# Where four operand splits and the feature splits stand in two engines' programs, at the start of a feed-forward stage

## The reference, cut to what matters

```python
h = rms_norm_2(x, norm2[l])
gate, up = jnp.split(h @ w_ffn_in[l], 2, axis=-1)
x = x + (jax.nn.silu(gate) * up) @ w_ffn_out[l]
return rms_norm_2(x, final_norm)
```

## Time and profile before

| | |
|---|---|
| median of 3 runs | 2473.76 us (2472.62 to 2474.74) |
| profiled execution, its own time | 2474.8 us |
| its span, first to last instruction | 2473.5 us |
| TensorE busy | 2366.0 us (96% of the span) |
| VectorE busy | 1412.2 us (57%) |
| ScalarE busy | 1138.8 us (46%) |
| GpSimd busy | 894.1 us (36%) |
| mean granted TensorE clock | 0.988 of full |

### The profile page before, as it was taken

The page is one execution under the profiler, slowest core; times in us unless marked ns, Lnnn a source line. Parts: engine busy times, 40 slices in busy tenths (PEclk is TensorE's granted clock), DMA queues, the critical chain, the costliest instruction groups (busy, mean ns, idle before and its releaser), DMA issues.

```text
span 2473.5 us, 31358 instructions
## 1 busy us (share of the span) xinstructions
PE 2366.0 (96%) x12068; PEld 1949.2 (79%) x12068; DVE 1412.2 (57%) x1963; ACT 1138.8 (46%) x1778; POOL 894.1 (36%) x665
## 2 busy tenths in 40 slices
PE   4999999989999999999999999999999999999998
PEld 3778788868888878876678877788877888888886
DVE  5255489958885240129973743332476666666665
ACT  4322288868884231239962474132333333333334
POOL 0111233336652212326521222012256655556551
PEclk8999999999999999999999999999999999999999
DMA  7234300000003131100021311013111111111111
GB/s 293 81 118 132 116 5 1 1 19 1 1 1 111 35 123 51 43 9 1 10 103 43 106 53 43 26 35 116 47 52 51 52 52 52 52 51 52 55 57 68
DMA packets 152488, 143.23 MB, mean 58 GB/s; under 512 B 10358, under 2 KB 140692, under 8 KB 150420
## 3 DMA queue, kind: packets, MB, share of 16 engines
q1 hardware_dynamic: 152340, 141.22, 18.1%
HBM read 124.43 MB, written 16.78 MB: 57 GB/s over the span
## 4 chain that ended last, share of the span: by engine, by line
PE 80%; ACT 8%; issue 5%; DVE 4%; POOL 2%; DMA 0%; SPq 0%; ACTq 0%; DVEq 0%; POOLq 0%
PE ps L260 37%; PE ps L2588 14%; PE ps L2605 9%; PE ps L1083 4%; PE ps L1106 3%; PE ps L1093 3%; ACT C_PR L1753 1%; PE ps L1642 1%; ACT B_PR L1166 1%; POOL WSL L2505 1%; ACT B_PTH L1160 1%; PE ps L2564 1%; PE ps L1621 1%; ACT C_PTH L1761 1%; PE ps L2032 1%
## 5 line engine op out<-in xcount | busy, mean ns | idle before, releaser
L249 POOL TENSOR_TENSOR WL<-WR,WH 128x1024 fp32r<-128x1024 f32 (+1 forms) x89 | 207.1, 2327 | 840.2 <-ACT WH L244 840.0
L260 PE MATMUL ps<-HH,WH 128*128 128x512 f32 (+1 forms) x1136 | 363.2, 401 | 3.3 <-POOL WL L249 1.7
L260 PE MATMUL ps<-HL,WH 128*128 128x512 f32 (+1 forms) x1136 | 353.4, 392 | 0.0
L260 PE MATMUL ps<-HH,WL 128*128 128x512 f32 (+1 forms) x1136 | 352.7, 392 | 0.0
L260 PEld LDWEIGHTS ps<-HH,WH 128*128 128x128 f32 (+1 forms) x1136 | 209.6, 189 | 56.2 <-issue 10.1
L260 PEld LDWEIGHTS ps<-HL,WH 128*128 128x128 f32 (+1 forms) x1136 | 213.8, 188 | 47.4
L260 PEld LDWEIGHTS ps<-HH,WL 128*128 128x128 f32 (+1 forms) x1136 | 213.7, 188 | 47.3
L2818 DVE TENSOR_TENSOR XF<-ps,XF 128x1024 f32<-128x1024 f32 x168 | 201.5, 1220 | 32.5 <-PE ps L2605 25.8
L2588 PE MATMUL ps<-HC,WSH 128*128 128x512 f32 x640 | 197.0, 389 | 0.0
L1119 DVE TENSOR_REDUCE NM<-ps 128x1 f32<-128x1024 f32 x128 | 156.1, 1220 | 35.0 <-PE ps L1083 34.1
L2505 POOL TENSOR_TENSOR WSL<-WSR,WSH 128x512 fp32r<-128x512 f32 x100 | 131.5, 1315 | 107.6 <-ACT WSH L2499 107.6
(11 more groups left out here) (432 smaller groups left out, 5217.1 us busy)
## 6 DMA issues: line engine op xcount, KB each, us to landing
WS<-in_w_ffn_in SPq DMA_DIRECT2D x44, 512.0 KB, 5.1
MKW<-in_ada_w SPq DMA_DIRECT2D x32, 512.0 KB, 4.1
spill<-X SPq DMA_DIRECT2D x3, 4096.0 KB, 13.6
OW<-in_w_ffn_out SPq DMA_DIRECT2D x22, 512.0 KB, 3.5
WR<-in_w_in SPq DMA_DIRECT2D x20, 512.0 KB, 3.9
WR<-in_odd_w_in SPq DMA_DIRECT2D x19, 512.0 KB, 3.8
WR<-in_even_w_in SPq DMA_DIRECT2D x17, 512.0 KB, 5.0
AWK<-in_ada_w SPq DMA_DIRECT2D x8, 1024.0 KB, 9.8
```

The lines of the kernel that those rows point to most:

```text
L249: pool.tensor_tensor(low[:, :, :], raw[:, :, :], high[:, :, :].bitcast(F32), ALU.subtract).then_inc(*w_low.up(t))
L260: last = pe.matmul(ps[0:w.m, 2 * s + h, :], wt[:, k, :], x[:, k, halves(h)], start=(k == 0 and n == 0), stop=(k == w.kt - 1 and n == 2))
```

## The change

Two groups of steps move within ScalarE's and VectorE's programs. No instruction is added, removed or resized, and TensorE's, GpSimd's and SyncE's programs stay.

```diff
@@ act_ffn
         act_silu(0)
         act_weight_high(1, 2)
         act_weight_high(1, 3)
-        act_operand_high(M3)
         act_a_high(0, 0)
         act_a_high(0, 1)
+        act_operand_high(M3)
         act_operand_high(M6)
@@ dve_ffn
         dve_operand_sum(M3)
         dve_operand_sum(M4)
-        dve_operand_low(M3)
         for j in range(NPLAIN):
             if j:
+                dve_operand_low(M3)
                 dve_operand_sum(M1)
                 for n in range(DT):
                     dve_y(j - 1, n)
@@
             dve_product(j, 1)
             dve_a_low(j, 0)
             dve_a_low(j, 1)
-        dve_operand_low(M4)
         for j in range(NPLAIN, NPAIR):
             for o in range(1, NPROD):
                 dve_after(j, o)
@@
                 if j == NPLAIN:
                     if o == M5:
+                        dve_operand_low(M4)
+                    elif o == M2:
                         dve_operand_low(M1)
-                    elif o == M2:
+                    elif o == M6:
                         dve_operand_sum(M7)
-                    elif o == M6:
+                    elif o == M4:
                         dve_operand_low(M7)
```

## The result

The changed kernel took 2477.38 us (median of 20 runs, 2471.02 to 2483.83), the kernel before 2474.27 us (20 runs). The medians lie 3.1 us apart. The measured ratio is 1.0017 with a 95% interval of 1.0009 to 1.0025, that is 4.2 us slower (2.2 to 6.2): a small loss, but clear of no change. The forecast was 2476.3 us.

What follows compares the result with a forecast made beforehand. TensorE, busy 2366.0 of 2473.5 us, was taken as the bound. With the -1.9 us gain inside, pair 2's ledgers gave +3.3 and +1.4; +2.5 was chosen and added to 2473.8: 2476.3 us, range 2471.3 to 2479.0.

Steps and rivals of the forecast that it cites:

- Gap (a): TensorE's wait ahead of y(0, 0) for ScalarE's AH; claimed to go whole, -1.9 us.
- Gap (b): TensorE's 3.0 us wait ahead of y(1, 2); claimed untouched, set by ScalarE's train of copies rather than VectorE, 0 us.
- The ledger: Step-by-step times of VectorE and TensorE through pair 2, with GpSimd's turns; y(2, 2) at 1884.1, +3.3 us.
- The turns with GpSimd: VectorE's split pairs at pair 2 waiting for GpSimd instructions; claimed 1.1 to 1.4 us each.
- the collision with the output weights: GpSimd's 2.41 us low part of OW ahead of low M7's first chunk; without it +1.4 us, with it +3.3.
- the full ledger: Pair 2's times with GpSimd's turns and the low part of OW ahead of low M7; claimed +3.3 us.
- the step down to +2.5: Choice for pair 2 between +3.3 us and +1.4 us, the case without the collision with OW.
- The clock, no price: At M7, a TensorE gap of 4.3 us was claimed to leave the clock alone; 0 us.
- R3: Slower: the wait at M7 halves TensorE's clock, +6.0 us or more; chance 0.11, shared with a longer debt.
- R1: The gain is kept, GpSimd's turns at pair 2 falling elsewhere; net -2.5 to -0.5 us, chance 0.22.
- R2: The wait ahead of y(1, 2) was VectorE's, held back by low M4; -4.9 to -6.3 us, chance 0.04.

Runs made afterwards that it cites:

- e1: Against the kernel before: only the moves of M3's high and low parts behind pair 0's features, pair 2 as before; ratio 0.9992 (0.9981 to 1.0003).
- e5: Against the kernel before: only VectorE's low M3 moved behind pair 0's low features, ScalarE's order as before; 2470.70 us, a single execution.
- e2: Against the kernel before: only pair 2's moves (low M4, low M1, sum M7, low M7), features as before; ratio 1.0020 (1.0006 to 1.0034).
- e7: Against the kernel before: first pair's half, plus ScalarE's high M1 behind its copies of M3 and M5 at pair 2; 2472.46 us, a single execution.
- e10: Against the changed kernel: 20 small matmuls put ahead of TensorE's wait at M7, to keep it awake; 2474.12 us, a single execution.
- e12: Against the changed kernel: low M4 and low M1 back in place, only sum M7 and low M7 late; ratio 1.0001 (0.9986 to 1.0017).
- e8: Against the kernel before: first pair's half, plus ScalarE's high parts and copies at pair 2 reordered; ratio 0.9994 (0.9983 to 1.0006).
- e9: Against e8: GpSimd's sums for M1 and M7 reordered, ScalarE's copies earlier in every pair from 2 on; ratio to before 0.9981 (0.9969 to 0.9992).
- e3: Against the changed kernel: low M4 back ahead of pair 2; low M1, sum M7 and low M7 stay late; 2477.07 us, a single execution.
- e4: Against the changed kernel: 26 small matmuls put ahead of TensorE's wait at M7, to keep it awake; 2482.07 us, a single execution.
- e6: Against the changed kernel: GpSimd's low part of pair 2's output weights behind pair 3's weights for M4; 2478.11 us, a single execution.
- e11: Against the changed kernel: sum M7 and low M7 back at their earlier steps, low M4 and low M1 stay late; 2475.87 us, a single execution.

## Why the prediction held, point by point

- **Gap (a), -1.9 us.** As forecast: y(0, 0) starts 27.3 us behind the first plain matmul (1807.01 - 1779.69) against 29.1 before, and y(1, 2) 68.4 against 70.3, 1.9 earlier. On its own (e1, e5) it brings D down by 1.5 to 2.7 us; what differs from 1.9 arises behind y(1, 2), in turns with GpSimd and in the clock.
- **Gap (b), 0 us.** The size was right, 2.86 us in both; so was the reason that it isn't VectorE's (e2), and for the changed kernel that it is ScalarE's train, with the sum for M7 1.1 us ahead of it. What I didn't see is that before the change GpSimd's sum ends within 0.1 us of that train, so that with low M4 in place a shorter train alone gains nothing (e7).
- **The ledger.** Its entries, moved by 1.7 us for the later first matmul, against the trace of after: "3+5" 1846.2 and 1846.23; low M4's end 1852.6 and 1852.55; low M1's end 1859.3 and 1859.06; M7's start 1871.1 and 1870.69; y(2, 2) 1885.8 and 1886.01. The turns with GpSimd and the collision with the output weights came as in the full ledger (+3.3, measured +3.5), so the step down to +2.5, taken between the ledgers, was the wrong one by 1.0 us. That the full ledger fits so well at y(2, 2) is partly luck: M7 began 0.4 us earlier than it said, and took 0.6 us longer.
- **The clock, no price.** That step failed. From the gap of 4.95 us I took that 4.3 us would leave the clock alone. It fell to the 1.2 GHz level (0.54 in the row), R3's mechanism, though for some 8 matmuls only. It cost 0.8 us (e10). The ledger had M7 at 3.8 us with the wait for its second chunk; at half clock that wait vanished into 4.4 us. Here the table of the Trainium skill that I had set aside ("TensorE: Matmul & The Clock Gate", "Why this matters for your kernels") was right about the gap ahead of M7. The rows of the opening were misread as well; see below the list.
- **R1** (gain kept) and **R2** (gap (b) was VectorE's) fall: D rose, and gap (b) stayed.
- **The rule of the Trainium skill on GpSimd and VectorE** ("GPSIMD Engine Reference", section 8: instructions with two SBUF inputs contend): the trace of after agrees, 3.44, 3.72 and 5.19 us beside GpSimd, 2.34 without it, and 2.34 or 2.35 for the additions from PSUM in pair 2, which GpSimd doesn't lengthen.

The opening again. The trace of before records no level of the clock ahead of 30.7 us, and the column shows 1.00 there even where TensorE does nothing (25 to 27 us). The pace of the matmuls shows the level. The 16 behind the gap of 4.95 us take 3.59 us; the same line's 16 ahead of it take as long, and 16 a little later about half:

```profile
18.71 3.62 PE L582 MATMUL ps<-IDENT,XIN 128*128 128x128 f32 x16
31.58 1.91 PE L582 MATMUL ps<-IDENT,XIN 128*128 128x128 f32 x16
```

Behind the gap 8 take 1.72 us, 0.215 us each, as 10 of the same size do in 2.14 us at clock 0.54. So by its pace TensorE was at the lower level on both sides of that gap, and the gap can't tell whether idle time makes the clock fall. The step rested on a row that didn't bear on it.

What stays open: of the 1.2 us between e1 and e5, whether the second turn of GpSimd came only because the slower clock had moved sum M7, and how far e12's D is the clock's. e8 and e9 each hold several edits, and which part of e9's gain comes from GpSimd's order and which from the copies of pair 3 wasn't tried apart.

## What to carry to other kernels

Work that sits in a hole of an engine is free only there: look at what its engine does on both sides of the move, in the idle time noted ahead of the next instructions, before taking a wait's name at its word. A wait named after one engine can be set by another's train two steps back, and by two trains at once, so that shortening one shows nothing (e7). And write the ledger with the full price of the collisions that the rows show.

## What the runs showed of the hardware that was not expected

The same idle time of 2.8 to 2.9 us ahead of y(1, 2) was followed by the full clock in before, after, e3 and e10, and by the lower level of the clock in e1, e2, e4, e5, e6, e7, e11 and e12 (two y in 4.4 to 5.3 us in place of 2.9). In e12 an idle time of 2.13 us ahead of M7 was enough:

```profile
1866.00:1868.30 2.30, 0.36 (x2) 1.00 0.11 11
1868.30:1872.00 3.70, 3.50 (x9) 0.57 0.39 135
```

So the length of one gap doesn't tell, in these runs, whether the clock falls; some of the scatter between single runs of one kernel may be this, which no run here isolates.

In the rows of pair 2 a VectorE instruction with two SBUF inputs and a GpSimd instruction take as long as if they never ran side by side and one waited for the other's whole turn. A pair of VectorE's chunks took 2.35 us with no GpSimd instruction beside it, 2.4 to 2.7 where only the end of one reached in, 3.4 to 3.9 with a whole one, 4.4 to 4.5 with two, and 5.2 to 5.5 with a long one among them.
